# One decoder step on one core: ScalarE counts half of the scores in four threshold searches, weight splits go behind page keys, norm diagonals one place ahead

## What is computed

```
x += 0.5 * SwiGLU1(RMSNorm(x))
z  = RMSNorm(x) @ w_in                        # q, k, v, indexer heads, conv parts
score[t,s] = sum_h w[t,h] relu(iq[t,h] . ik[s])   for s <= t
keys of token t = the 256 best scores (lax.top_k), softmax attention over these alone
x += concat(attn, conv) @ w_out
x += 0.5 * SwiGLU2(RMSNorm(x))
x += sigmoid(RMSNorm(x) @ w_ple_gate) * (p @ w_ple_proj)
y  = RMSNorm(x)
```

## Time and profile before

| | us |
|---|---|
| median of 3 runs | 2883.78 |
| lowest and highest | 2875.74, 2886.01 |
| the profiled execution, its own time | 2886.01 |
| its span in the trace | 2884.2 |
| PE busy in the span | 2613.6 (91%) |
| DVE, ACT, POOL busy | 1314.1, 1000.5, 1013.2 |

### The profile page before, as it was taken

The page is one execution under the profiler, slowest core; times in us unless marked ns, Lnnn a source line. Parts: engine busy times, 40 slices in busy tenths (PEclk is TensorE's granted clock), DMA queues, the critical chain, the costliest instruction groups (busy, mean ns, idle before and its releaser), DMA issues.

```text
span 2884.2 us, 40451 instructions
## 1 busy us (share of the span) xinstructions
PE 2613.6 (91%) x15166; PEld 2284.0 (79%) x15166; DVE 1314.1 (46%) x3141; ACT 1000.5 (35%) x1637; POOL 1013.2 (35%) x527
## 2 busy tenths in 40 slices
PE   6999998988879888899989976889999999999997
PEld 6999997768657677777776876778889897878786
DVE  3222324438763443353565877764333233332344
ACT  4222224622223333345444212444443333332332
POOL 4333333223443333322343332221223444454340
PEclk9999998999989888899999987999999999999998
DMA  4333333322324344311322221111112322333221
GB/s 158 104 106 93 94 109 125 113 87 81 108 88 131 114 122 126 95 59 45 114 74 74 73 67 44 45 44 45 52 45 81 102 81 95 95 104 99 84 66 70
DMA packets 157029, 253.33 MB, mean 88 GB/s; under 512 B 15009, under 2 KB 101282, under 8 KB 156834
## 3 DMA queue, kind: packets, MB, share of 16 engines
q1 hardware_dynamic: 154144, 247.02, 27.0%
q10 hardware_dynamic: 2690, 3.72, 0.4%
HBM read 240.34 MB, written 18.73 MB: 90 GB/s over the span
## 4 chain that ended last, share of the span: by engine, by line
PE 72%; DVE 13%; ACT 4%; issue 4%; POOL 3%; DVEq 2%; DMA 1%; ACTq 0%; SPq 0%
PE ps L1453 22%; PE ps L1454 20%; PE ps L1455 20%; PE ps L1666 2%; PE ps L1722 2%; DVE hits L1252 1%; POOL w_lo L744 1%; DVE hits_late L1252 1%; PE ps L1652 1%; DVE s_hits L1302 1%; DVE ps L1102 1%; PE ps L1588 1%; POOL d_lo L744 1%; DVE ha_lo L1104 1%; ACT w_hi L845 1%
## 5 line engine op out<-in xcount | busy, mean ns | idle before, releaser
L744 POOL TENSOR_TENSOR w_lo<-raw,w_hi 128x1024 fp32r<-128x1024 f32 x250 | 604.5, 2420 | 1025.7 <-ACT w_hi L845 1025.2
L1453 PE MATMUL ps<-xna_hi,w_hi 128*128 128x288 f32 x2000 | 612.3, 306 | 23.6 <-POOL xna_lo L750 6.1
L1454 PE MATMUL ps<-xna_lo,w_hi 128*128 128x288 f32 x2000 | 600.4, 300 | 0.0
L1455 PE MATMUL ps<-xna_hi,w_lo 128*128 128x288 f32 x2000 | 600.1, 300 | 0.0
L1453 PEld LDWEIGHTS ps<-xna_hi,w_hi 128*128 128x128 f32 x2000 | 387.3, 194 | 38.7 <-issue 16.8
L1453 PE MATMUL ps<-xnb_hi,w_hi 128*128 128x512 f32 x1000 | 410.6, 411 | 0.0
L744 POOL TENSOR_TENSOR d_lo<-raw,d_hi 128x1024 fp32r<-128x1024 f32 x90 | 215.7, 2417 | 552.1 <-ACT d_hi L845 552.1
L1454 PE MATMUL ps<-xnb_lo,w_hi 128*128 128x512 f32 x1000 | 397.9, 398 | 0.0
L1455 PE MATMUL ps<-xnb_hi,w_lo 128*128 128x512 f32 x1000 | 397.4, 397 | 0.0
L1454 PEld LDWEIGHTS ps<-xna_lo,w_hi 128*128 128x128 f32 x2000 | 386.9, 193 | 0.2
L1455 PEld LDWEIGHTS ps<-xna_hi,w_lo 128*128 128x128 f32 x2000 | 386.2, 193 | 0.0
(11 more groups left out here) (291 smaller groups left out, 4046.8 us busy)
## 6 DMA issues: line engine op xcount, KB each, us to landing
raw<-in_w_gu SPq DMA_DIRECT2D x176, 512.0 KB, 3.5
raw<-in_w_d SPq DMA_DIRECT2D x88, 512.0 KB, 3.5
raw<-in_w_ring SPq DMA_DIRECT2D x74, 512.0 KB, 3.5
pages<-in_vk_pages SPq DMA_DIRECT2D x256, 128.0 KB, 2.6
idx_flat<-in_idx_pages SPq DMA_DIRECT2D x256, 32.0 KB, 2.3
idxp<-idx_flat SPq DMA_DIRECT2D x8, 1024.0 KB, 7.7
x_spill<-xa SPq DMA_DIRECT2D x1, 2304.0 KB, 8.9
xa<-x_spill SPq DMA_DIRECT2D x4, 576.0 KB, 5.9
```

Source lines behind the costliest of these rows:

```text
L744: g_.tensor_tensor(lo[slot][:, :, :], raw[l % 2][:, :, :], hi[slot][:, :, :].bitcast(f32), ALU.subtract).then_inc(lo_done, 1)
L1453: mm(out, shi, mhi, start=first, stop=False)
L1454: mm(out, shi, mlo, start=False, stop=False)
L1455: return mm(out, slo, mhi, start=False, stop=last)
```

## The change

Six edits.

1. **Samples' search.** VectorE counts columns 0 to 1023 of a step and ScalarE the other 1032: `Sign` of candidate minus score, summed by the same instruction (`sample_signs`). The candidates of all steps are kept. VectorE decides bit j-1 at event j, when ScalarE's sum has come.
2. **B1 and B2.** VectorE counts the first block of the two (640 or 896 columns), ScalarE the second by signs (768 or 1024). Search A stays.
3. A sum of signs counts an equal score as half. So the 32nd choice is followed by a correction: the lowest candidate that was dropped (`lowest_dropped`) is counted once more with "at least" and taken if it holds (`take_dropped`), on VectorE, in "sties" 0 and in `places_left`.
4. **Splits behind keys.** `with_weights` holds a split event back while "ks" events follow, so at the end of a product `K_hi` and `kv_kr` come ahead of the weights' `w_hi` and `w_lo`.
5. **Places.** The samples' search stands in spots 2 to 41 (before 2 to 53), the attention from spot 43 (before 55).
6. **Norms and `vtr`.** The diagonals are an event of their own, one place ahead of "spread"; the second transpose of `vtr(0)` goes to PSUM bank 7 and waits for the ninth evacuation of the sample scores by ScalarE, no longer for the last "scale" of chunk 2's norm.

```diff
-        groups = [[("sums", k, c)], [], [("spread", k, c)] + ...
+        groups = [[("sums", k, c)], [("diag", k, c)], [("spread", k, c)] + ...
...
-        first = weave(first, groups + units + [[], [("mix", 0)], [("back", 0)]], 55, -2)
-        ev += weave(first, search, 2, 54)
+        first = weave(first, groups + units + [[], [("mix", 0)], [("back", 0)]], 43, -2)
+        ev += weave(first, search, 2, 42)
...
         def split(slot, *name):
             self.pos[name] = len(self.items)
             self.items.append((slot, name))
-            out.append(("sp", len(self.items) - 1))
+            held.append(("sp", len(self.items) - 1))
         for e in events:
+            if e[0] != "ks":
+                out += held
+                held.clear()
...
+            def sample_signs(j):
+                act.wait_ge(s_cand_ready, j + 1)
+                A(s_hits[:, COUNTED:HW], S0[:, COUNTED:HW], ACT.Sign, bias=s_cands[:, j:j + 1].bitcast(f32), scale=-1.0,
+                  accum_out=s_extra[:, 0:1]).then_inc(s_signs_added, 1)
+
+            def signs(name, j):
+                if name != "A":
+                    b, q = SEARCH[name][1], 32 * (name == "B2") + j + 1
+                    act.wait_ge(b_cand_ready, q)
+                    A(hits_of(name, j)[b][:, :], sc(b), ACT.Sign, bias=b_cands[:, j:j + 1].bitcast(f32), scale=-1.0,
+                      accum_out=b_extra[:, 0:1]).then_inc(b_signs_added, 1)
...
-            def spread(k, c):
+            def diagonals(k, c):
...
+            def shared_bit(name, j):
+                if j == 0:
...
+                else:
+                    shared_choice(name, j - 1)
...
+                dve.drain().then_inc(b_cand_ready, 1)
+                count(hits_of(name, j), SEARCH[name][:1], cand[:, :].bitcast(f32), ALU.is_ge)
+
+            def shared_choice(name, j):
+                k, weight = 128 * (SEARCH[name][1] + 1), float(2 ** (31 - j)) if j else -1.0
+                dve.wait_ge(b_signs_added, 32 * (name == "B2") + j + 1)
+                dve.drain()
+                v.tensor_scalar(drop[:, 0:1], reached[:, 0:1], TOPK - 0.5, weight, ALU.is_lt, ALU.mult)
+                v.tensor_scalar(b_drops[:, j:j + 1], b_extra[:, 0:1], k - 2 * TOPK + 1.5, weight, ALU.is_gt, ALU.mult)
+                dve.drain()
...
             def places_left(name):
+                if name != "A":
+                    b = SEARCH[name][1]
+                    shared_choice(name, 31)
+                    lowest_dropped(b_cands, b_drops, b_extra)
+                    v.tensor_scalar(hits_of(name, 31)[b][:, :], sc(b), b_extra[:, 2:3], None, ALU.is_ge, ALU.add, accum_out=b_extra[:, 1:2])
...
+                    take_dropped(cand[:, 1:2], drop[:, 1:2], b_extra)
...
             def sample_bit(j):
...
+                else:
+                    sample_bit_choice(j - 1)
+                dve.drain().then_inc(s_cand_ready, 1)
+                v.tensor_scalar(s_hits[:, 0:COUNTED], S0[:, 0:COUNTED], s_cands[:, j:j + 1].bitcast(f32), None, ALU.is_ge, ALU.add, accum_out=s_reached[:, :])
...
+            def sample_bit_choice(j):
+                dve.wait_ge(s_signs_added, j + 1)
+                dve.drain()
+                v.tensor_scalar(s_extra[:, 1:2], s_extra[:, 0:1], -0.5, s_reached[:, :], ALU.mult, ALU.add)
+                dve.drain()
+                other_half(s_extra[:, 1:2])
+                v.tensor_scalar(s_drops[:, j:j + 1], s_other[:, :], s_extra[:, 1:2], TOPK - 0.5 - (HW - COUNTED), ALU.add, ALU.is_lt)
+                dve.drain()
...
             def sample_choice(part):
                 if part == 0:
+                    sample_bit_choice(31)
+                    lowest_dropped(s_cands, s_drops, s_extra)
+                    v.tensor_scalar(s_hits[:, :], S0[:, :], s_extra[:, 2:3], None, ALU.is_ge, ALU.add, accum_out=s_reached[:, :])
...
             def spread(k, c):
-                pe.wait_ge(diag_done, n("spread", k, c))
+                pe.wait_ge(diag_done, n("diag", k, c))
...
                 if g == 0:
                     pe.wait_ge(si_relu, 18)
-                    pe.wait_ge(xnf_done, n("scale", 0, 2, KT - 1))
+                    pe.wait_ge(si_evac, 9)
...
-                    last = transpose(ps[:, 6, 0:128], vT[0][:, 0:NS], ident[:, 0, :])
+                    last = transpose(ps[0:NS, 7, 0:128], vT[0][:, 0:NS], ident[:, 0, :])
```

More of the change, by code:

```diff
@@ L173, in norm @@
     def norm(self, k, c, apart=False):
-        groups = [[("sums", k, c)], [], [("spread", k, c)] + [("scale", k, c, m) for m in range(4)], [("scale", k, c, m) for m in range(4, KT)]]
+        groups = [[("sums", k, c)], [("diag", k, c)], [("spread", k, c)] + [("scale", k, c, m) for m in range(4)], [("scale", k, c, m) for m in range(4, KT)]]
         return groups if apart else [e for g in groups for e in g]
@@ L235, in order @@
         second = flat(squares(0, 1))
[L236 removed]
+        ev = [("begin",)] + flat(squares(0, 0)) + [("weights", 0), ("sums", 0, 0), ("diag", 0, 0)] + second[:4] + [("spread", 0, 0)]
         ev += scales(0, 0, range(4)) + second[4:] + scales(0, 0, range(4, KT)) + [("weights", 1)]
         first = self.two_chunks(0, range(FT))
[L240 removed]
+        ev += first[:1] + [("sums", 0, 1), ("diag", 0, 1)] + first[1:2] + [("spread", 0, 1)] + scales(0, 1, range(KT))
         first = first[2:]
@@ L245, in order @@
         last = self.down(0, PAIRS - 1, 1, 1)
-        ev += last[:6] + [("sums", 1, 0)] + last[6:] + [("spread", 1, 0)] + [("scale", 1, 0, m) for m in range(KT)]
+        ev += last[:6] + [("sums", 1, 0), ("diag", 1, 0)] + last[6:] + [("spread", 1, 0)] + [("scale", 1, 0, m) for m in range(KT)]
         ev += [("spill", 0), ("rtab", 0), ("il", 0), ("il", 1)]
@@ L303, in order @@
         end = len(first) - 4
-        ev += first[:end] + [("sums", 4, 0)] + first[end:] + [("spread", 4, 0)]
+        ev += first[:end] + [("sums", 4, 0), ("diag", 4, 0)] + first[end:] + [("spread", 4, 0)]
         ev += [("scale", 4, 0, m) for m in range(KT)] + [("y", 0)] + self.norm(4, 1) + [("y", 1)]
@@ L310, in with_weights @@
         self.items, self.pos = [], {}
-        out = []
+        out, held = [], []
         def split(slot, *name):
@@ L336, in with_weights @@
                         split(("d", s), "pp", s)
-        return out
+        return out + held
     def ends(self, e):
@@ L1254, in threshold_bit @@
             def threshold_bit(name, j):
-                blocks = SEARCH[name]
+                if name != "A":
+                    return shared_bit(name, j)
                 if j == 0:
@@ L1436, in mix @@
                     v.tensor_tensor(xn_lo[g][:, j, :], attn[g][:, j, :], xn_hi[g][:, j, :].bitcast(f32), ALU.subtract).then_inc(mixa_ready, 1)
-            does = {"begin": begin, "sq": square, "sums": sums, "spread": spread, "scale": scale, "p": product, "d": add,
+            does = {"begin": begin, "sq": square, "sums": sums, "diag": diagonals, "scale": scale, "p": product, "d": add,
                     "iw": head_weights, "prep": prepare, "wm": head_matrix, "isc": index_scores, "bt": threshold_bit,
```

79 lines of the change are left out of this document (57 added, 22 removed).

## The result

The changed kernel takes 2814.2 us (median of 4 runs, 2810.72 to 2818.35) against 2879.88 us before (median of 4): a ratio of 0.9771, with a 95% interval of 0.9745 to 0.9797. That is 65.7 us less; the forecast was 2800 us, 83 less than the profiled execution before. The two profiled executions stand further apart, 2886.01 and 2810.72, because the first is at the slow end of its runs and the second at the fast end. A difference of one stretch between two traces is therefore good to some 4 us.

What follows compares the result with a forecast made beforehand. TensorE, busy 91% of the span, bounds the kernel, so savings elsewhere count where it waits or its clock is low. Terms −25 −8 −25 −25 = −83 give 2803 us profiled, 2801 against the median, said as 2800; range 2745 to 2860.

Steps and rivals of the forecast that it cites:

- Diagonals, −25: Norms: diagonals made one place earlier remove most of PE's 39.5 us of waits for them; 25 us saved, bounds 15 and 35.
- `vtr`, −8: Transpose of vtr(0): PE's 6.93 us wait for chunk 2's last scaled tile goes; 8 us saved, bounds 3 and 10.
- The search, −20 at its end: Samples' search: shorter steps save 15.4, one down moved out 11, the correction costs 6; it ends 20 us earlier.
- 0.7 a step, 22 steps: Samples' search: sharing each count with ScalarE saves 0.7 us a step over 22 steps, 15.4 us.
- Moved work and keys, −24 or −25 for 690 to 1400: Search −20, attention −14, prompt blocks +10: −24, rounded to −25; bounds 0 and −65.
- The return of edit 4: Attention: of 34 us of kv_kr waits removed, 10 us come back because w_lo, raw loads and pages are later.
- Rival (a): Attention: page waits in SP's queue replace key waits, so keys ahead of splits gains nothing; 2834 us, chance 0.20.
- Its sign: Attention: K_hi waiting for pages much over 28 us would show that pages had taken the place of the keys.
- edit 4's price: Attention: eleven PE waits for kv_kr at product ends, 34 us, go when keys come ahead of splits.
- B1 and B2, −25: Searches B1 and B2: ScalarE's share saves 8 in B1's late steps, 15 in B2, 2 by clock; bounds +10 and −45.
- Rival (c): Searches: weight splits in ScalarE's queue delay sums of signs, VectorE's choice and PE; 2921 us, chance 0.08.
- The rule on table loads: Search steps: Sign outside the tables of SiLU and Exp would cost one or two loads, 1.3 to 2.6 us; not expected.

Runs made afterwards that it cites:

- norms_old: Changed kernel with the diagonals made at the spread event again and vtr(0)'s second transpose in bank 6 behind the last scale: 2834.3 us (0.9826).
- places_old: Changed kernel with the samples' search back in spots 2 to 53 and the attention from spot 55: 2811.0 us (0.9743).
- pages_first: Changed kernel with SP issuing the raw block's load behind the next pages' loads: 2788.0 us (0.9670).
- pages_splits_first: Changed kernel with pages ahead of raw loads on SP, but splits ahead of keys again: 2824.1 us (0.9788).
- b_dve: Changed kernel with VectorE counting both blocks of B1 and B2 again, no signs or correction there: 2822.6 us (0.9780).
- places_31: Changed kernel with pages ahead of raw loads, splits behind the samples' and B1's signs, search and attention another 12 spots ahead: 2778.3 us (0.9639).

## Why the prediction was right, and where its terms were off

The direction, the size and the range held. The terms, in the order of the sum:

- **Diagonals, −25.** Between 16 and 19 by `norms_old`. The mechanism was right (waits 38.6 and 16.0, where I said under 12); five waits stayed, the largest of them 4.9 us, 7.6 before. The waits fell by some 23 us; the term was too large because I counted them as time and PE's waits for other parts of the norms took some 5 back.
- **`vtr`, −8.** The wait of 6.9 us is gone and is back in `norms_old`; with the low clock around it (0.72 from 634 to 652 us there, 1.00 from 634 to 648 in the changed kernel) some 9.
- **The search, −20 at its end.** It is 24, but from other sources than I had: 22 by the places and 2 by the signs. The step that failed is "0.7 a step, 22 steps": the steps are 0.74 shorter when nothing disturbs them, but a late raw block and the downs, where VectorE's adds go at PE's pace, take half of it. The correction then takes 4.0 where I had 6, and PE stands still for it.
- **Moved work and keys, −24 or −25 for 690 to 1400.** The stretch from 690 to the norm went from 745.2 to 719.4, −26. That this meets the −25 is luck, since its parts are off and cancel: edit 4 gave 15 instead of 24, the keys took no less time than before, where I had −14, and the rest −1 where I had +10. The moved work cost less than the 20 and 10 that I counted, 7 to 10 and 6 to 7 by `places_old`. In the rest the difference to −1 stands in `places_old` too (215.7 us for the same matmuls that took 223.4 before, at a clock of 0.98 for 0.95); which edit gave it is open. The return of edit 4 was mis-sized, 20 for 10. Rival (a) named the right queue and the right cause, the raw load that stands ahead of the pages; `pages_first` and `pages_splits_first` show it. Its sign, `K_hi` waiting for pages much over 28 us, came true with 77.8, and `kv_kr`'s waits fell to 27.4 and not to about 10. It took over half of edit 4's price, not all of it.
- **B1 and B2, −25.** −18 in the two traces, 14.7 by `b_dve`. B2 came out at the 15 that I counted for it (12 by `b_dve`). B1's late steps gave 3 to 4 of 8, although an undisturbed step takes 1.82 us where I expected 2.05 (in B2 2.03 where I expected 2.3): the wait shown above costs 7 and another 4. Rival (c) is these waits; they stand at two places in B1's late steps, where ten splits lie, so ScalarE's queue did not become the lockstep.
- **The rule on table loads.** The Trainium skill, "ScalarE: Activation LUTs", section "Table sets: the hidden batching unit", asks for a load where a function of another set comes in between. The trace has 97 table loads of 1.283 us where there were 95, and none stands with a sum of signs, so no run here shows that price. A sum takes 1.156 us for 1032 columns with 0.187 for the read, as long as the 1.34 taken from the earlier trace rows.

The medians moved by 65.7 us where the terms, undone one at a time, make 26 (norms), 15 (B1 and B2), 6 (signs), about 10 by the ratios (keys) and 0 to 8 (places): 57 to 65. The intervals, some 7 us to either side, are too wide to say more than that nothing large is missing.

## What to carry to other kernels

When an order on one queue is changed to free an engine, look at what the delayed instruction itself releases: here `w_lo` freed a buffer, the load of which stood on SP ahead of the pages that the freed engine needed next. Take such a load, with its wait, behind the transfers that don't depend on it, before judging the first change. Work that a stretch can't use, because another engine sets its pace, can be moved to a stretch with waits, but count what it costs there: here 14 to 17 of the 22 us came back, and what was left is at the edge of what the timing tells.

## What the runs showed of the hardware that was not expected

The clock made up part of the gains (17 of the 35 us that edit 4 is worth with the pages in front) and was not steady between executions of the same code: the key products had a granted clock of 0.93 in one execution of the changed kernel and 0.92 in another, 0.90 in `b_dve`, where only later work differs, and took 365, 368 and 373 us. With the pages in front and more products among the keys (`places_31`), PE's waits for `kv_kr` were 11.6 us, the clock 0.97, and 42 matmuls more than in the changed kernel went through in 28 us less. So in this stretch a wait taken away was worth more than its own length: 25 us less for `kv_kr` made it 35 us shorter.
